# A decoder trunk's attention output projection: from four plain weight slots to the seven products of Strassen's algorithm

## The chip, the cores and the metric

The kernel is one program on one NeuronCore of a Trainium2 chip. The metric is the device time of one execution in microseconds; several runs are taken and the median is shown. The profile is one further execution, recorded instruction by instruction. The engines are TensorE (PE: matmuls and transposes), VectorE (DVE), ScalarE (ACT), GpSimd (POOL) and SyncE (SP, which issues the loads). They run in parallel and wait for each other through semaphores.

## The reference, cut to what matters

Two layers over 512 rows of width 1024. Layer 0 has two head groups (sparse softmax attention `o_a`, gated linear attention `o_b`), layer 1 a convolution module. The change concerns the last line of layer 0; its result is normed and is the input of layer 1.

```python
h = rmsnorm(x, norm_even[i]);  proj = h @ w_in_even[i]
...
o_a = dsa_attention(...).reshape(B, S, A_W) * jax.nn.silu(ga)      # 512 x 512
o_b = (rms-normed gla(...) * gla_norm).reshape(B, S, B_VW) * jax.nn.silu(gb)   # 512 x 512
x = x + jnp.concatenate([o_a, o_b], axis=-1) @ w_out_even[i]      # (512 x 1024) @ (1024 x 1024)
...
h = rmsnorm(x, norm_odd[j])
proj = h @ w_in_odd[j]
val, glu_g, gate = _split(proj, ODD_SPLIT)
```

## The kernel before, in words

Matmuls are made in three passes of rounded 32-bit operands: each operand is split into a high part (its rounding) and a low part (the rest), and high x high, high x low and low x high are summed in PSUM. So every weight has to be split before use. Weights come in slots of 1 MB (128 partitions x 2048 columns), listed by `plan_slots` (line 86) and numbered j. For each slot SyncE loads `w_raw[j % 2]` (`load`, line 452: it waits until the low part of slot j - 2 is made), ScalarE rounds it into `w_hi[j % 3]` (`split_hi`, line 729: it waits until TensorE has done with slot j - 3), and GpSimd subtracts into `w_lo[j % 3]` (`split_lo`, line 568). Each engine has its own program in a fixed order; nothing overtakes.

Slots 0 to 15 are the even layer's input projection, with the attention's and the linear attention's work put in between by hand. GpSimd's loop over slots (line 672) also holds the differences of the gated attention's levels (`diff`, line 630; levels "k", 64, 32, ...), which ScalarE exponentiates and VectorE multiplies for TensorE.

Slots 16 to 19 (`S_OE` up to `S_ODD`) are the output projection: two column halves of 512, each in two slots of 512 rows of the weight. First TensorE transposes the mixed rows `oa`, `ob` (32 blocks of 128x128, line 1529), ScalarE and VectorE make their high and low parts from PSUM (`hT_high`, `hT_low`), and then `unit_b` (line 1614) makes 12 matmuls of 128x512 for each of four row tiles in each slot. VectorE adds a finished tile to x (`add_rows`, line 1337), ScalarE takes squares (`row_squares`, line 896), VectorE makes the variance, GpSimd the reciprocal root (`rsqrt`, in its loop at step 19 ahead of the split of slot 21), VectorE scales the rows (`scale_rows`). TensorE transposes row tiles 0 and 1 of the normed x (`odd_rows(0)`, 16 transposes) before the very last unit of slot 19, and tiles 2 and 3 within the first odd slot, 20. That slot's matmuls (`group_half`, line 1890) wait chunk by chunk for the low parts of those rows, which follow the high parts (`half_high`, line 747).

GpSimd's order around the stage: split of 18, of 19, of 20 (the first odd slot), four `rsqrt`, a wait for all normed rows, split of 21.

## Time and profile before

| | us |
|---|---|
| median of 3 runs (lowest to highest) | 517.46 (517.19 to 517.59) |
| the profiled execution | 517.29 |
| its span, first to last instruction | 515.6 |
| TensorE matmul busy | 505.2 (98%), 2855 instructions |
| VectorE, ScalarE, GpSimd busy | 358.7, 244.6, 295.6 |
| mean granted TensorE clock | 0.998 of full |

The span is what the profile's rows cover; 1.69 us of the execution lie outside it. A busy TensorE is not one at its peak, as matmuls are pipelined: the distance between starts tells their cost.

### The profile page before, as it was taken

The page shows a single profiled execution, that of the slowest core. Times are in us where ns is not written, and L with a number is a line of the kernel's source. Part 1 is how long each engine was busy: PE and PEld are TensorE (multiplying, and loading weights), DVE is VectorE, ACT ScalarE, POOL GpSimd, SP SyncE. Part 2 cuts the span into 40 slices and gives each one's busy share as a digit, 9 for nine tenths or more (in the row PEclk, how much of TensorE's full clock was granted, in tenths as well). Part 3 has the DMA queues.
Part 4 walks back from the last instruction along what each step waited for, and adds up shares of the span by engine and source line. Part 5 has one row for each costly group of instructions (what it writes and reads, how often), then busy time and mean ns, then how long its engine had stood idle before and what let it go on. Part 6 is the DMA issues. An engine that isn't in the chain of part 4 may idle for free.

```text
span 515.6 us, 7658 instructions
## 1 busy us (share of the span) xinstructions
PE 505.2 (98%) x2855; PEld 408.0 (79%) x2855; DVE 358.7 (70%) x742; ACT 244.6 (47%) x407; POOL 295.6 (57%) x184
## 2 busy tenths in 40 slices
PE   7999999999999999999999999999999999999994
PEld 7866888788888888888898889888677777788883
DVE  3795599759966556647470136699999999849814
ACT  6734844232221244554271335648666665447303
POOL 5470755737734067556506404797999999950701
PEclk9999999999999999999999999999999999999999
DMA  8443355222222002100082220636877763502004
GB/s 272 116 153 124 123 164 164 84 83 83 83 73 92 1 0 83 51 32 1 10 317 83 82 82 0 164 83 158 203 195 184 185 162 106 175 31 81 1 0 163
DMA packets 47474, 54.73 MB, mean 106 GB/s; under 512 B 4424, under 2 KB 32099, under 8 KB 47438
## 3 DMA queue, kind: packets, MB, share of 16 engines
q1 hardware_dynamic: 47438, 54.25, 35.4%
q8 instruction: 22, 0.36, 0.3%
q14 instruction: 14, 0.11, 0.1%
HBM read 50.37 MB, written 3.72 MB: 105 GB/s over the span
## 4 chain that ended last, share of the span: by engine, by line
PE 86%; DVE 9%; ACT 3%; issue 1%; POOL 0%; POOLq 0%; ACTq 0%
PE bank L1608 33%; PE bank L1628 29%; PE bank L1826 3%; PE bank L1753 3%; DVE r_va L1147 2%; PE bank L1803 2%; PE bank L1917 2%; DVE top L1145 2%; PE bank L1904 2%; PE bank L1815 2%; DVE r_ob L1131 1%; PE bank L1644 1%; PE bank L1543 1%; PE bank L1692 1%; PE bank L1770 1%
## 5 line engine op out<-in xcount | busy, mean ns | idle before, releaser
L577 POOL TENSOR_TENSOR w_lo<-w_raw,w_hi 128x2048 fp32r<-128x2048 f32 (+1 forms) x31 | 140.4, 4529 | 99.6 <-ACT w_hi L739 98.6
L1608 PE MATMUL bank<-hT_lo,w_hi 128*128 128x512 f32 (+1 forms) x280 | 110.7, 395 | 0.0
L1608 PE MATMUL bank<-hT_hi,w_hi 128*128 128x512 f32 (+1 forms) x280 | 110.4, 394 | 0.0
L1608 PE MATMUL bank<-hT_hi,w_lo 128*128 128x512 f32 (+1 forms) x280 | 110.1, 393 | 0.0
L1628 PE MATMUL bank<-w_hi,hT_hi 128*128 128x512 f32 x252 | 101.9, 404 | 0.0
L1628 PE MATMUL bank<-w_hi,hT_lo 128*128 128x512 f32 x252 | 98.4, 391 | 0.0
L1628 PE MATMUL bank<-w_lo,hT_hi 128*128 128x512 f32 x252 | 98.3, 390 | 0.0
L739 ACT ACTIVATE w_hi<-w_raw 128x2048 fp32r<-128x2048 f32 (+1 forms) x35 | 65.7, 1880 | 40.3 <-PE bank L1628 35.3
L1401 DVE SCALAR_TENSOR_TENSOR bank<-r_va,pvec,bank 128x512 f32<-128x512 f32 x94 | 69.1, 753 | 2.2
L1608 PEld LDWEIGHTS bank<-hT_lo,w_hi 128*128 128x128 f32 (+1 forms) x280 | 52.3, 187 | 16.3 <-issue 5.7
L1608 PEld LDWEIGHTS bank<-hT_hi,w_hi 128*128 128x128 f32 (+1 forms) x280 | 52.3, 187 | 12.8 <-issue 1.5
L1608 PEld LDWEIGHTS bank<-hT_hi,w_lo 128*128 128x128 f32 (+1 forms) x280 | 52.3, 187 | 11.8 <-issue 1.0
L1628 PEld LDWEIGHTS bank<-w_hi,hT_hi 128*128 128x128 f32 x252 | 47.4, 188 | 11.9 <-issue 2.2
L1628 PEld LDWEIGHTS bank<-w_hi,hT_lo 128*128 128x128 f32 x252 | 47.3, 188 | 10.1
L1628 PEld LDWEIGHTS bank<-w_lo,hT_hi 128*128 128x128 f32 x252 | 47.4, 188 | 8.6
L658 POOL TENSOR_TENSOR r_g<-r_g 128x512 f32<-128x512 f32 x40 | 50.5, 1296 | 5.5 <-ACT r_g L938 5.5
L609 POOL TENSOR_TENSOR r_g<-r_x,neg_mask 128x128 f32<-128x128 f32 (+3 forms) x32 | 25.4, 798 | 39.7 <-DVE row_max L1257 36.6
L791 ACT ACTIVATE r_g<-r_g,neg_max 128x128 f32<-128x128 f32 (+3 forms) x32 | 17.9, 561 | 48.4 <-PE bank L1815 38.6
L1401 DVE SCALAR_TENSOR_TENSOR bank<-r_qkb,pvec,bank 128x512 f32<-128x512 f32 x48 | 35.2, 753 | 1.0
L565 POOL TENSOR_TENSOR rstd<-stat,minus_half 128x1 f32<-128x1 f32 (+1 forms) x13 | 9.6, 743 | 44.6 <-DVE stat L1044 40.3
L1282 DVE COPY r_g<-bank 128x128 f32<-128x128 f32 (+3 forms) x32 | 15.7, 491 | 22.1 <-PE bank L1815 21.9
L1340 DVE TENSOR_TENSOR r_x<-bank,r_x 128x512 f32<-128x512 f32 x8 | 5.5, 689 | 29.8 <-PE bank L1628 29.8
(240 smaller groups left out, 793.4 us busy)
## 6 DMA issues: line engine op xcount, KB each, us to landing
w_raw<-in_w_in_even_dram SPq DMA_DIRECT2D x14, 1024.0 KB, 5.2
w_raw<-in_w_in_odd_dram SPq DMA_DIRECT2D x16, 512.0 KB, 5.1
w_raw<-in_w_out_even_dram SPq DMA_DIRECT2D x4, 1024.0 KB, 8.3
w_raw<-in_w_in_odd_dram SPq DMA_DIRECT2D x4, 1024.0 KB, 7.9
w_raw<-in_w_out_odd_dram SPq DMA_DIRECT2D x4, 1024.0 KB, 5.0
r_att<-u_kept SPq DMA_DIRECT2D x12, 258.0 KB, 4.3
r_ka<-u_kept SPq DMA_DIRECT2D x12, 258.0 KB, 4.5
r_x<-in_x_dram SPq DMA_DIRECT2D x4, 512.0 KB, 6.0
```

The costliest lines, as they stand in the source:

```text
L577: nc.gpsimd.tensor_tensor(v(w_lo[j % 3]), v(w_raw[j % 2]), v(w_hi[j % 3]).bitcast(F32), ALU.subtract).then_inc(lo_ready, 1)
L609: nc.gpsimd.tensor_tensor(masked[n % 2][:, 0:w], bias_cols(h, w), neg_mask[:, MASK_AT[tb]:MASK_AT[tb] + w], ALU.add).then_inc(masked_ready, 1)
L658: nc.gpsimd.tensor_tensor(acc[i % 2], acc[i % 2], prod[((POOL_TAPS - 2) * c + i) % 3], ALU.add).then_inc(pool_added, 1)
L739: nc.scalar.activation(v(w_hi[j % 3]), v(w_raw[j % 2]), ACT.Copy).then_inc(hi_ready, 1)
L791: nc.scalar.activation(prob[n % 2][:, 0:w], logit[n % 2][:, 0:w], ACT.Exp, bias=neg_max[:, n:n + 1], accum_out=row_sum[:, n:n + 1]).then_i ...
L1145: ins = nc.vector.max(top8[:, tb - 1, :], score[tb])
L1282: nc.vector.tensor_copy(probT[n % 2][:, 0:w], bank[6][:, 0:w]).then_inc(probT_ready, 1)
L1401: ins = nc.vector.scalar_tensor_tensor(out=acc, in0=u, scalar=w, in1=acc, op0=ALU.mult, op1=ALU.add)
L1608: ins = nc.tensor.matmul(proj_bank(g)[0:m, :], w[:, k, P * i:P * i + m], h[:, k, :], start=(n == 0), stop=(n == 3 * KC - 1))
L1628: ins = nc.tensor.matmul(proj_bank(g)[:], h[:, k, P * t:P * t + P], w[:, i, :], start=(first and i == 0 and q == 0), stop=(final and i == ...
L1753: ins = nc.tensor.matmul(bank[4 + (n + i) % 4][:, n_q * t:n_q * t + n_q], keys, queries, start=True, stop=True)
L1826: ins = nc.tensor.matmul(bank[7][:, AD * h:AD * h + AD], probT[n % 2][:, P * i:P * i + P], va[:, i, AD * h:AD * h + AD], start=(i == 0), s ...
```

## The change

The rows are divided into an early half (tiles 0 and 1) and a late half (tiles 2 and 3), the columns into a (`oa`) and b (`ob`), and `w_out_even` into four quadrants B11, B12, B21, B22 of 512x512. Strassen's algorithm in its form with few sums, with some signs turned, makes seven products of 256x512 by 512x512 where four pairs (eight) were made: late b x B11, late a x B21, s1 x (B11 + B12), s2 x (B11 + B12 + B22), s3 x (B12 + B22), early a x (B11 + B12 + B21 + B22), s4 x B22, with s3 = late b - early b, s2 = - early a - s3, s1 = - s2 - late b, s4 = s1 - late a + late b. They accumulate in banks 2, 3, 6 and 7, and VectorE adds a bank to, or subtracts it from, tiles of x 14 times where there were 8 additions. Each product is a slot: 16 to 22. The odd layer's slots move from 20 to 23 and so on; `S_ODD` is 23.

The four sums of weights are made in device memory: SyncE copies quadrants (DRAM to DRAM), GpSimd issues six transfers that add onto them. Slots 18 and 19 are loaded from there to `w_raw`; slots 20, 21 and 22 (two sums and B22) go to `r_att`, `r_qa` and `r_ka`, early. The load of x moves behind slot 19's. The high parts of s1 to s4 are ScalarE's; the low parts of s3 and s1 are GpSimd's, between its splits of slots 18 and 19; the other sums and low parts are VectorE's. Only slot 16's and 17's splits stay within the attention. The order of the odd norm is rewritten: the squares of six half tiles stand between ScalarE's splits, and the four `rsqrt` stand behind GpSimd's split of slot 23. The diff, cut to its core:

```diff
+MIX = ("late b", "late a", "s1", "s2", "s3", "early a", "s4")
...
-    s += b("oe", 0, B_FIRST) + b("oe", 512, B_FIRST)
+    s += [("s", up[4:8], [(0, "oe", 0, 512)]), ("s", up[0:4], [(0, "oe", 0, 512)]), ("t", up[0:4], [(0, 0, 0, 512)]),
+          ("t", up[0:4], [(0, 1, 0, 512)])] + [("t", (), [])] * 3
...
+    B11, B12, B21, B22 = (WSRC["oe"][r:r + 512, c:c + 512] for r, c in ((512, 0), (512, 512), (0, 0), (0, 512)))
...
+        def raw(j):
+            if S_OE + 4 <= j < S_ODD:
+                return (r_att, r_qa, r_ka)[j - S_OE - 4][:, 0:2048]
...
+                if kind == "t":
+                    for _, n, _, _ in pieces:
+                        sp.wait_ge(lo_ready, j - 1)
+                        load_quadrant(w_raw[j % 2][:], t_sum[n], t_summed[n], (16, 32)[n], raw_in[j % 2])
+                    return
...
+                if j == 5:
+                    for i, q in enumerate((B11, B11, B12, B11)):
+                        sp.dma_start(t_sum[i], q).then_inc(t_begun, 16)
...
+                if j == S_OE + 3:
+                    sp.wait_ge(logit_ready, NSTEP)
+                    sp.dma_start(x_t, x[0].rearrange("(t p) d -> p t d", p=P)).then_inc(x_again, 16)
+                    sp.wait_ge(qk_done, NSTEP)
+                    load_quadrant(r_qa[:], t_sum[3], t_summed[3], 32, late_in[1])
+                    sp.dma_start(r_ka[:, 0:2048].rearrange("p (k n) -> p k n", k=4),
+                                 B22.rearrange("(k p) n -> p k n", p=P)).then_inc(late_in[2], 16)
...
+            def add_to(n, src):
+                nc.gpsimd.dma_start(t_sum[n], src, accum_op=ALU.add).then_inc(t_summed[n], 16)
...
+            def low_of_s3():
+                pool.wait_ge(mix_hi, 7)
+                pool.wait_ge(s2_ready, 2)
+                nc.gpsimd.tensor_tensor(s3_lo, s3, s3_hi.bitcast(F32), ALU.subtract).then_inc(s_low, 1)
+            def low_of_s1():
+                pool.wait_ge(mix_hi, 8)
...
-                if s_ == S_OE + 3:
+                if s_ == S_OE + 1:
+                    low_of_s3()
+                    low_of_s1()
+                if s_ == S_ODD - 1:
                     for t in range(TB):
...
+                if s_ == 3:
+                    pool.wait_ge(t_begun, 64)
+                    add_to(0, B12)
+                    add_to(1, B12)
+                    add_to(2, B22)
+                    add_to(3, B21)
+                if s_ == 5:
+                    pool.wait_ge(t_summed[2], 16)
+                    pool.wait_ge(t_summed[1], 16)
+                    pool.wait_ge(t_summed[3], 16)
+                    add_to(1, B22)
+                    add_to(3, t_sum[2])
...
+            for n in range(2):
+                act.wait_ge(mixed_T, n + 1)
+                nc.scalar.activation(hT_hi[:, 4 + 2 * n:6 + 2 * n, HALF:S], two_chunks(n), ACT.Copy,
+                                     scale=b_norm).then_inc(mix_hi, 1)
+                nc.scalar.activation(late_b[:, 512 * n:512 * n + 512], bank[n][:], ACT.Copy,
+                                     scale=b_norm).then_inc(late_kept, 1)
+            for n in range(2):
+                act.wait_ge(mixed_T, 5 + n)
+                nc.scalar.activation(hT_hi[:, 2 * n:2 * n + 2, 0:HALF], two_chunks(4 + n), ACT.Copy).then_inc(mix_hi, 1)
+            split_hi(S_OE + 2)
+            for n in range(2):
+                act.wait_ge(mixed_T, 7 + n)
+                nc.scalar.activation(hT_hi[:, 2 * n:2 * n + 2, HALF:S], two_chunks(n), ACT.Copy).then_inc(mix_hi, 1)
+            act.wait_ge(s3_ready, 2)
+            nc.scalar.activation(s3_hi, s3, ACT.Copy).then_inc(mix_hi, 1)
+            split_hi(S_OE + 3)
+            act.wait_ge(s1_ready, 2)
+            nc.scalar.activation(hT_hi[:, 4:KC, 0:HALF], s1.rearrange("p (c t) -> p c t", c=4), ACT.Copy).then_inc(mix_hi, 1)
+            for n in range(2):
+                cols = slice(512 * n, 512 * n + 512)
+                nc.scalar.activation(s2_hi[:, cols], bank[4 + n][:], ACT.Copy).then_inc(mix_hi, 1)
+            split_hi(S_OE + 4)
+            act.wait_ge(s4_ready, 4)
+            for n in range(2):
+                cols = slice(512 * n, 512 * n + 512)
+                nc.scalar.activation(s4_hi[:, cols], bank[n][:], ACT.Copy).then_inc(mix_hi, 1)
+            split_hi(S_OE + 5)
...
+            mix_square(2, 0, 0, 3)
+            mix_square(3, 0, 1, 4)
+            split_hi(S_OE + 6)
+            mix_square(0, 1, 2, 9)
+            mix_square(1, 1, 3, 10)
+            split_hi(S_ODD)
+            mix_square(0, 0, 4, 11)
+            mix_square(1, 0, 5, 12)
+            split_hi(S_ODD + 1)
+            mix_square(2, 1, 6, 13)
+            act.wait_ge(mix_unit, 12)
+            half_high(R_ODD, 0, odd_bank, odd_row)
+            mix_square(3, 1, 7, 14)
+            half_high(R_ODD, 1, odd_bank, odd_row)
...
+            def mix_add(b, t, half, unit):
+                dve.wait_ge(mix_unit, unit)
+                xs = x_t[:, t, 512 * half:512 * half + 512]
+                nc.vector.tensor_tensor(xs, xs, bank[b][:], ALU.subtract if half else ALU.add).then_inc(mix_added, 1)
...
+                dve.wait_ge(mixed_T, 3 + n)
+                nc.vector.scalar_tensor_tensor(out=s3[:, cols], in0=bank[2 + n][:], scalar=minus_norm, in1=late_b[:, cols],
+                                               op0=ALU.mult, op1=ALU.add).then_inc(s3_ready, 1)
+            for n in range(2):
+                low_of_chunks(4 + n, slice(2 * n, 2 * n + 2), EARLY, 3 + n)
+            for n in range(2):
+                cols = slice(512 * n, 512 * n + 512)
+                dve.wait_ge(s3_ready, n + 1)
+                dve.wait_ge(mix_low, 3 + n)
+                nc.vector.scalar_tensor_tensor(out=bank[4 + n][:], in0=bank[4 + n][:], scalar=-1.0, in1=s3[:, cols],
+                                               op0=ALU.mult, op1=ALU.subtract).then_inc(s2_ready, 1)
+            for n in range(2):
+                low_of_chunks(n, slice(2 * n, 2 * n + 2), LATE, 5 + n)
+            for n in range(2):
+                cols = slice(512 * n, 512 * n + 512)
+                dve.wait_ge(s2_ready, n + 1)
+                nc.vector.scalar_tensor_tensor(out=s1[:, cols], in0=bank[4 + n][:], scalar=-1.0, in1=late_b[:, cols],
+                                               op0=ALU.mult, op1=ALU.subtract).then_inc(s1_ready, 1)
+            for n in range(2):
+                cols = slice(512 * n, 512 * n + 512)
+                dve.wait_ge(s1_ready, n + 1)
+                dve.wait_ge(mix_low, 5 + n)
+                nc.vector.tensor_tensor(bank[n][:], s1[:, cols], bank[n][:], ALU.subtract).then_inc(s4_ready, 1)
+            for n in range(2):
+                cols = slice(512 * n, 512 * n + 512)
+                dve.wait_ge(s4_ready, n + 1)
+                nc.vector.tensor_tensor(bank[n][:], bank[n][:], late_b[:, cols], ALU.add).then_inc(s4_ready, 1)
+            dve.wait_ge(x_again, 16)
+            mix_add(6, 2, 0, 1)
+            for n in range(2):
+                cols = slice(512 * n, 512 * n + 512)
+                low_of_bank(4 + n, s2_lo[:, cols], s2_hi[:, cols], 9 + n)
+            mix_add(7, 3, 0, 2)
+            dve.wait_ge(mix_added, 2)
+            mix_add(2, 2, 0, 3)
+            mix_add(3, 3, 0, 4)
+            mix_add(2, 0, 1, 5)
+            for n in range(2):
+                cols = slice(512 * n, 512 * n + 512)
+                low_of_bank(n, s4_lo[:, cols], s4_hi[:, cols], 11 + n)
+            mix_add(3, 1, 1, 6)
+            mix_add(6, 2, 1, 7)
+            mix_add(7, 3, 1, 8)
+            dve.wait_ge(mix_added, 6)
+            mix_add(6, 0, 1, 9)
+            mix_add(7, 1, 1, 10)
...
+            def mix_variance(t):
+                last = 1 if t >= 2 else 0
+                dve.wait_ge(half_squares, 5 + t)
+                nc.vector.scalar_tensor_tensor(out=stat[:, t:t + 1], in0=half_sq[:, TB * last + t:TB * last + t + 1],
+                                               scalar=1.0 / D, in1=stat[:, t:t + 1], op0=ALU.mult,
+                                               op1=ALU.add).then_inc(var_ready, 1)
...
+            mean_square(2)
+            mean_square(3)
+            mix_add(6, 0, 0, 11)
+            mean_square(0)
+            mean_square(1)
+            mix_variance(0)
+            mix_add(7, 1, 0, 12)
             scale_rows(0, TB + 1)
-            row_variance(1, 0, 1)
+            mix_variance(1)
             scale_rows(1, TB + 2)
+            dve.wait_ge(mix_added, 8)
+            mix_add(2, 2, 1, 13)
...
+            FREED = {"s2": 1, "s1": 3, "s3": 7, "early a": 9, "s4": 5}
...
+                if name == "late a":
+                    pe.wait_ge(s3_ready, 2)
+                elif name in FREED:
+                    pe.wait_ge(mix_added, FREED[name] + t)
+                b = bank[MIX_BANK[name] + t]
+                wh = w_hi[j % 3][:].rearrange("p (k n) -> p k n", k=4)
+                wl = w_lo[j % 3][:].rearrange("p (k n) -> p k n", k=4)
+                pe.wait_ge(mix_hi, HIGH[name])
+                for q in range(3):
+                    if q == 1:
+                        slot_ready(j)
+                    if q == 2:
+                        if name in LOW:
+                            pe.wait_ge(mix_low, LOW[name])
+                        else:
+                            pe.wait_ge(s_low, LOW_S[name])
+                    for i in range(4):
+                        hi, lo = mix_operand(n, i, t)
+                        ins = nc.tensor.matmul(b[:], lo if q == 2 else hi, (wl if q == 1 else wh)[:, i, :],
+                                               start=(n < 3 and q == 0 and i == 0), stop=(q == 2 and i == 3),
+                                               skip_group_check=True)
+                ins.then_inc(mix_unit, 1)
...
+            quad_transposes(4, 2, 0)
+            quad_transposes(4, 0, 2)
+            pe.wait_ge(mixed_a, 1)
+            quad_transposes(0, 0, 4)
...
+            for n in range(len(MIX)):
+                pe.wait_ge(hi_ready, S_OE + n)
+                for t in range(2):
+                    if n == 0 and t == 1:
+                        pe.wait_ge(mix_low, 2)
+                        pe.wait_ge(late_kept, 2)
+                        pe.wait_ge(mixed_a, 2)
+                        quad_transposes(0, 2, 0)
+                        pe.wait_ge(oa_emptied, TB)
+                    if n == len(MIX) - 1 and t == 1:
                         odd_rows(0)
-                    unit_b(s_, t, hT_base=R_MIX if s_ < S_OE + 2 and t == 0 else None)
+                    mixed_unit(n, t)
```

## Rows read from the trace of the kernel before

**Rows 1.** The page, parts 1 and 4: busy us (share) by engine, and the chain's shares.

```profile
PE 505.2 (98%) x2855; PEld 408.0 (79%) x2855; DVE 358.7 (70%) x742; ACT 244.6 (47%) x407; POOL 295.6 (57%) x184
...
PE 86%; DVE 9%; ACT 3%; issue 1%; POOL 0%; POOLq 0%; ACTq 0%
```

**Rows 2.** The chain that ended last, in order of time: start us, us, what.

```profile
263.29 3.50 PE bank L1533 x32
266.79 40.83 PE bank L1628 x180
310.24 0.87 DVE hT_lo L1058 x2
313.73 3.59 PE bank L1904 x27
```

**Rows 3.** Timeline of GpSimd: start us, us, engine, line, operation [idle before].

```profile
271.07 4.60 POOL L577 TENSOR_TENSOR w_lo<-w_raw,w_hi 128x2048 fp32r<-128x2048 f32 x1 [16.99 <-ACT w_hi L739]
290.67 4.62 POOL L577 TENSOR_TENSOR w_lo<-w_raw,w_hi 128x2048 fp32r<-128x2048 f32 x1 [6.27 <-ACT w_hi L739]
304.01 0.56 POOL L565 TENSOR_TENSOR rstd<-stat,minus_half 128x1 f32<-128x1 f32 x1 [8.71 <-DVE stat L1044]
306.66 0.55 POOL L565 TENSOR_TENSOR rstd<-stat,minus_half 128x1 f32<-128x1 f32 x1 [2.09 <-DVE stat L1044]
```

**Rows 4.** Timeline of ScalarE, the changed stretch.

```profile
264.81 2.42 ACT L744 ACTIVATE hT_hi<-bank,pb 128x512 fp32r<-128x512 f32 x4 [2.96 <-PE bank L1533]
269.02 1.98 ACT L739 ACTIVATE w_hi<-w_raw 128x2048 fp32r<-128x2048 f32 x1
309.39 3.01 ACT L751 ACTIVATE hT_hi<-bank,pvec 128x256 fp32r<-128x256 f32 x8
```

**Rows 5.** Timeline of VectorE, the changed stretch.

```profile
264.67 0.69 DVE L1313 TENSOR_TENSOR r_oa<-r_oa,r_qkb 128x512 f32<-128x512 f32 x1
268.18 2.48 DVE L1050 SCALAR_TENSOR_TENSOR hT_lo<-bank,hT_hi 128x512 fp32r<-128x512 f32 x4
305.55 0.47 DVE L1032 TENSOR_SCALAR r_oa<-r_x,rstd 128x512 f32<-128x512 f32 x1
```

**Rows 6.** Timeline of GpSimd at the start: splits of 1024 columns.

```profile
9.07 2.38 POOL L614 TENSOR_TENSOR w_lo<-w_raw,w_hi 128x1024 fp32r<-128x1024 f32 x1 [1.09 <-ACT w_hi L766]
11.90 2.90 POOL L614 TENSOR_TENSOR w_lo<-w_raw,w_hi 128x1024 fp32r<-128x1024 f32 x1 [0.45 <-ACT w_hi L770]
```

**Rows 7.** Line 464's loads (two each): landing times, 275-277 and 320.5-324 us.

```profile
DMA to landing us min/median/max: 4.0/4.6/5.2
...
DMA to landing us min/median/max: 3.8/5.1/6.4
```

**Rows 8.** Timelines of VectorE (three rows), GpSimd and TensorE, 87 to 120 us.

```profile
90.20 2.11 DVE L1167 COPY chunk_decay<-r_oa 128x8 f32<-128x8 f32 x1
110.65 0.66 DVE L1178 TENSOR_TENSOR r_g<-r_g,r_qkb 128x512 f32<-128x512 f32 x1
118.72 1.86 DVE L1178 TENSOR_TENSOR r_g<-r_g,r_qkb 128x512 f32<-128x512 f32 x1
...
87.67 4.62 POOL L577 TENSOR_TENSOR w_lo<-w_raw,w_hi 128x2048 fp32r<-128x2048 f32 x1 [5.76 <-ACT w_hi L739]
...
96.42 0.66 PE L1719 MATMUL bank<-ident,r_g 128*128 128x128 f32 x4 [0.43 <-DVE r_g L1175]
```

**Rows 9.** Page part 6, timeline of ScalarE, and line 1753's instructions, 100 to 120.

```profile
w_raw<-in_w_in_even_dram SPq DMA_DIRECT2D x14, 1024.0 KB, 5.2
...
84.24 0.60 ACT L756 ACTIVATE r_vb<-bank 128x512 f32<-128x512 f32 x1 [2.12 <-PE bank L1628]
...
L1753 PE MATMUL bank<-r_g x32: 272/272/320, 114.6 to 116.4; 64*128 64x64 f32 x32
```

**Rows 10.** Stretches of the start: busy us by engine, granted clock, DMA, GB/s.

```profile
0.00:2.00 2.00, 0.00 (x0) 0.00 (x0) 0.27 (x1) 1.21 (x1) 1.05 (x9) 1.00 0.19 23
2.00:4.00 2.00, 1.31 (x13) 1.34 (x14) 0.29 (x1) 0.08 (x1) 1.31 (x7) 1.00 0.86 320
```

More of the change, by code:

```diff
@@ L148, in sb, with shared @@
             return ctx.enter_context(nc.sbuf_tensor(name, shape, dt))
+        def shared(name, shape):
+            with nc.sbuf_tensor(name, shape, F32) as plain:
+                pass
+            return plain, sb(name + "_split", shape, F32R)
         def sem(name):
@@ L271, in hybrid_trunk @@
         u_kept = nc.dram_tensor("u_kept", [2, P, KEPT], F32, kind="Internal").ap()
+        t_kept = nc.dram_tensor("t_kept", [2, 512, 1024], F32, kind="Internal").ap()
+        t_sum = [t_kept[i // 2][:, 512 * (i % 2):512 * (i % 2) + 512] for i in range(4)]
         bias_rows = nc.dram_tensor("bias_rows", [AH, S + P], F32, kind="Internal").ap()
@@ L286, in hybrid_trunk @@
         x_again = sem("x_again")
+        t_begun = sem("t_begun")
+        t_summed = [sem(f"t_summed{i}") for i in range(4)]
+        late_in = [sem(f"late_in{i}") for i in range(3)]
+        mixed_T = sem("mixed_T")
+        mix_hi = sem("mix_hi")
+        mix_low = sem("mix_low")
+        s_low = sem("s_low")
+        late_kept = sem("late_kept")
+        s1_ready = sem("s1_ready")
+        s2_ready = sem("s2_ready")
+        s3_ready = sem("s3_ready")
+        s4_ready = sem("s4_ready")
+        mix_unit = sem("mix_unit")
+        mix_added = sem("mix_added")
         nf_in = sem("nf_in")
@@ L1528, in _ @@
             pe.wait_ge(pool_chain, 2)
-            def transpose_blocks(order, blocks, ready, bank_of):
-                for n, t in blocks:
-                    ready(n, t)
-                    ins = nc.tensor.transpose(bank[bank_of(n)][:, P * t:P * t + P], hx(t, order[n]), ident[:])
-                    if t == TB - 1:
-                        ins.then_inc(hT_in_bank, 1)
-            LOW, HIGH = range(4), range(4, KC)
-            ROWS_1 = [(n, t) for part in (LOW, HIGH) for t in range(TB) for n in part]
             def keep_clock(n, dst):
@@ L1617, in unit_b @@
                 ks = SLOTS[j][1]
-                first, final = j % 2 == 0, j % 2 == 1
+                first, final = j in BEGINS, j not in BEGINS
                 if first and part[0] == 0:
@@ L1860, in _, with quad_transposes @@
             pv(NSTEP - 1)
[L1862 to L1871 removed]
+            def quad_transposes(first_chunk, first_t, first_bank):
+                for n in range(2):
+                    for c in range(2):
+                        for t in range(2):
+                            at = HALF * c + P * t
+                            ins = nc.tensor.transpose(bank[first_bank + n][:, at:at + P],
+                                                      hx(first_t + t, first_chunk + 2 * n + c), ident[:])
+                    ins.then_inc(mixed_T, 1)
```

168 lines of the change are left out of this document (96 added, 72 removed).

## The prediction

> **What bounds the kernel now.** I read the page first: TensorE is busy 98% of the span and holds 86% of the chain that ended last [rows 1]. So time is lost or won where TensorE's instructions are fewer, or where it is made to wait. Next the chain of waits over the changed stretch [rows 2]: 32 transposes take 263.29 to 266.79 us, then matmuls of 128x512 run without a gap. 180 of them take 40.83 us, so one costs 0.2268 us. The stretch ends with a wait on VectorE: the low part of the odd layer's transposed rows is late, and TensorE resumes at 313.73. Third, the timelines of the other engines. GpSimd splits a weight slot in 4.60 us and has long pauses [rows 3]; ScalarE splits one in 1.9 to 2.0 us and starts the odd layer's high parts at 309.39 [rows 4]; VectorE's 512-column step costs 0.69 us, and 0.62 from start to start when nothing is waited for [rows 5]. Slots here are numbered as in the plan; slot 23 after the change is what slot 20 was (the odd layer's first).
>
> **TensorE's saving.** Before: 4 slots x 4 row tiles x 12 = 192 matmuls. After: 7 products x 2 tiles x 12 = 168. The 32 transposes and the 16 of the odd rows stay. So 24 x 0.2268 = 5.44 us less, if nothing waits. A product takes 24 x 0.2268 = 5.44 us, and a slot serves TensorE for 5.44 us where it served 10.9: the other engines get half the time for each slot, and three slots more.
>
> **The start.** The first transposes begin at 263.1 (the chain gives 263.29, as it counts them from the end of the matmuls before). ScalarE may start a copy of a bank about 0.25 us after its last transpose was due, as at 264.81 [rows 4]. Six copies at 0.55 us follow (high and kept late b, twice; high early a, twice), 263.8 to 267.1, then the split of slot 18 to 269.0. Product 1 needs the second high part (265.5), so it starts at 265.8, as soon as 24 transposes are out; its second tile follows the last 8 transposes and ends at 272.1. Product 2 ends at 277.55. Its low parts are ready in time (271.9 against 274).
>
> **A first wait, about 1.5 us.** Product 3 starts anew in bank 2, so TensorE waits until VectorE has made its third addition to x. VectorE's queue from 265.3: 2 lows, 2 of s3, 2 lows, 2 of s2, 2 lows, 2 of s1, 4 of s4, one addition, 2 lows, 2 additions, 21 steps. At 0.62 us each, with a pause of 0.25 for ScalarE's second kept copy and 0.1 for each of two own waits, they end at 278.8. TensorE resumes at 279.0 instead of 277.55. Bounds: 0.9 us if no step pauses (265.3 + 13.0 = 278.3), 3.5 us if each takes 0.74, a whole 0.69 and a latency (280.8). I take the low side, since steps that don't wait for the one before start 0.62 apart in the rows. Beyond 2.3 us this wait would also push GpSimd's queue, below.
>
> **The wait that decides: GpSimd's queue before the odd rows.** The rsqrt of each row of the odd norm stands in GpSimd's order behind the split of the odd layer's first slot (23), as it did before behind slot 20, which was done at 290.67 + 4.6 [rows 3], 9 us early. Now the queue is: slot 18 (from 269.1), low of s3, low of s1, slots 19, 20, 21. Weight splits are 4.60; the two lows are 128x1024, of which the trace has one at 2.38 and one at 2.90 [rows 6]; I take 2.38, as nothing else holds the port there. 269.1 + 4.6 + 2 x 2.35 + 3 x 4.6 = 292.2. The high parts it needs come in time: slot 20's after product 2 (279.8), slot 21's after product 3, which ends at 284.5 (286.8, GpSimd free 287.6). Only when slot 21 is split does SyncE load slot 23, since a load waits for the low part two slots back. Two pieces of 512 KB, issued 0.5 us apart; the second lands 5.2 us after issue in the one row and 6.4 in the other [rows 7]. With 5.2 (three other odd slots have 5.1 to 5.4): 292.3 + 0.5 + 5.2 = 298.0. ScalarE splits it to 300.0, GpSimd to 304.7. Meanwhile products 4 to 6 end at 289.9, 295.35 and 300.8, and the first tile of product 7 at 303.5; there TensorE turns to the odd rows and must wait for them.
>
> One step more. VectorE's mix_variance(0) reads three operands in SBUF at about 300.8, while GpSimd splits slot 23. The trace shows that such steps wait for a running GpSimd instruction: the copy of 128x8 of line 1167 starts at 90.20, takes 2.11 us and ends where GpSimd's split of 87.67 + 4.62 ends, and the same kind of multiplication takes 0.66 us at 110.65, where GpSimd pauses, and 1.86 at 118.72, under a split [rows 8]. So mix_variance(0) and the addition queued behind it (number 12, which ScalarE's square and the norm of row 1 wait for) go at 304.7. The Trainium skill ("SBUF — State Buffer", Who interferes with whom) says the same: VectorE with two SBUF inputs and a GpSimd instruction that reads SBUF take turns on a shared port, and whichever came first blocks the other. By that rule my end is 0.3 us later than if the two could overlap.
>
> So: rsqrt(0) 304.9 to 305.5; addition 12 to 305.5; square to 306.4; scaling of row tile 0 to 306.4; variance, rsqrt(1) to 307.3 (0.6 us each, [rows 3]); scaling of row tile 1 (0.40 a half, [rows 5]) to 308.2. TensorE's 16 transposes end at 308.8 instead of 305.25: a second wait of 3.55 us. Its last tile ends at 311.5, which no longer matters, since the odd layer waits for VectorE and ScalarE: addition 13 at 308.8, its square to 309.6, then the high parts of the odd rows from 309.6, where they began at 309.39 before [rows 4]. From there the order is as before, and TensorE resumes at 313.9 against 313.73 [rows 2].
>
> The sum of the stage: -5.44 + 1.5 + 3.55 = -0.4 at TensorE's last tile (311.5 against 311.9), and then +0.6, because the low parts are waited for: +0.2 us.
>
> **The additions in device memory.** SyncE issues four 1 MB copies behind slot 5's load (at 39 us); GpSimd then adds onto them four times (behind slot 5's split, 64.75), waits for three of the four behind its split of slot 7, and issues two more. No row shows a copy from DRAM to DRAM or an addition. Copies: slot 6 is loaded at 58.1, behind them, and TensorE wants it when slot 5 is done, about 84 (its last bank is emptied at 84.24 [rows 9]); less two splits it may land as late as 77.5, so they may take till 72, 33 us for four. A load alone is 5.2 us [rows 9]; four make 21, and 42 if a copy costs a load and a store. Queued back to back a megabyte goes in 3.3 us (320 GB/s in [rows 10]), so 13, or 26 for load and store. The nearest row is a queue of loads, so I take the copies as hidden; at 42 slot 6 would land at 86 and TensorE lose 8 us, which belongs to rival 3. Additions: each reads two megabytes and writes one. If each costs two of those 3.3 us, four cost 26 and the slots' own loads 7: done near 98. If each costs three, near 111. GpSimd's split of slot 8 (87.67 [rows 8]) and the difference for level 64 stand behind that wait; TensorE wants the level at 114.6 [rows 9] and it needs 10 us from the release (split 4.6, difference 2.1, exponential 1.1, two products 1.3, latencies), so the breaking point is 104. I take no loss, with a rival for the other end. There is a gain too: if GpSimd's splits leave 90 to 96 us, the blocked copy and multiplications of VectorE there go quicker, and TensorE's wait of 0.43 us at 96.42 [rows 8] is gone. Take -0.4 (bounds 0 and -0.9, the weight load's wait there). The issues themselves: 0 to 1 us each of GpSimd, in pauses of about 5 us (5.8 before slot 8's split). The Trainium skill ("DMA: Bandwidth & Descriptors", Issuing engines are not separate DMA queues) has the additions share the 16 engines with SyncE's loads; no row here shows it.
>
> The one VectorE step for the minus sign (0.15 us in its pause) and SyncE's earlier wait for ob_summed (190 us, next load at 197.8) are free.
>
> **Sum.** 517.29 (profiled execution, 515.6 of span and 1.69 around it) + 0.2 - 0.4 = 517.1; the median shown is 0.17 higher, so 517.3.
>
> **The rivals.**
> 1. GpSimd's queue is not the end that decides (its steps run quicker, or another order). Then the variances follow the additions: rsqrt(1) near 303.6, high parts from 306.1 instead of 309.39: -3.3, 514.0. For it: before, slot 20's low part was there 9 us early. Against: each term is a row. 0.22.
> 2. Nothing waits at all, 5.44 less: 511.9. Against it are 21 VectorE steps in one queue. 0.04.
> 3. Slower: additions in device memory hold GpSimd beyond 104 us. Price: the time over 104, one for one; at three loads' cost 111, so 7 us; I write 521.3 for a typical 4. For it: the least known rate of all. 0.17.
> 4. Slower: both uncertain ends of the queue are the long ones, lows of 2.90 (+1.0) and a landing of 6.4 (+1.2): 519.4. 0.07.
> 5. Slower: the clock. TensorE idles about 2.6 us before the odd rows. The longest idle before has 2.7 us, at the very start, and the granted clock reads 1.00 there [rows 10]. If it fell to 1.2 GHz, the last tile would cost 2.7 us more, of which 2.3 are covered by the wait for the low parts; with a few half-speed matmuls of the odd layer +1.5: 518.8. 0.08. The Trainium skill ("TensorE: Matmul & The Clock Gate", Part 1) says that throttled is the default and activity releases it; by that rule such a gap is a risk.
> 6. The forecast, with its own range of 516.2 to 518.6: 0.42.
>
> **Numbers.** A difference under 0.2%, 1.0 us, is what a measurement of this kernel can't tell from none. The forecast's 0.42 is 0.36 within, 0.03 on either side. Faster 0.22 + 0.04 + 0.03 = 0.29; slower 0.17 + 0.07 + 0.08 + 0.03 = 0.35; same 0.36. The range runs from just below rival 1 to rival 3's typical price: 513.8 to 521.5.
>
> **What would show it.** TensorE: 168 matmuls of the mix, a wait of 1 to 2 us before product 3 released by VectorE's addition to x, and one of 3 to 4 us before the odd transposes, released by a scaling that waited for rsqrt, behind GpSimd's split of slot 23. GpSimd without a pause from 269 to 292. The high parts of the odd rows at 309.6 relative to transposes at 263.1. Wrong if the odd rows' transposes follow product 7's first tile at once, if GpSimd's split of slot 8 starts after 104, or if the granted clock falls below 1.00 in the stretch.

## The result, and the profile after

The changed kernel takes 533.39 us (median of 4 runs, 532.96 to 534.05) against 517.43 beside it: a ratio of 1.031, 95% interval 1.0297 to 1.0323, so 15.96 us slower. The forecast was 517.3, and its range ended at 521.5. The profiled execution has a span of 531.7 us against 515.6.

The page first, parts 1 and 4, as in [rows 1]: TensorE has 24 matmuls less and 95% instead of 98% of the span, and DMA stands in the chain, where it had no share.

```profile
PE 504.1 (95%) x2831; PEld 405.5 (76%) x2831; DVE 369.8 (70%) x761; ACT 254.0 (48%) x416; POOL 319.5 (60%) x195
...
PE 75%; DMA 8%; POOL 6%; ACT 4%; issue 3%; DVE 2%; SPq 0%; POOLq 0%; ACTq 0%; DVEq 0%
```

Where that share lies, the chain of waits shows for 60 to 120 us (start us, us, what). One addition in device memory takes 33.39 us, and everything until TensorE's matmul at 112.55 hangs on it.

```profile
66.64 33.39 DMA t_kept<-in_w_out_even_dram
...
101.22 1.41 POOL t_kept L673
102.63 4.52 POOL w_lo L636
107.15 0.99 POOL r_g L723
108.14 1.02 POOL r_g L724
109.18 1.06 ACT r_g L873
110.27 0.69 DVE r_g L1304
110.96 0.60 DVE r_g L1305
111.56 0.94 DVE r_oa L1315 x2
112.50 0.04 issue
112.55 1.12 PE bank L1930 x8
```

The same stretch in the timelines of the engines (idle time before an instruction, and what ended it, stand in brackets): TensorE, then GpSimd, then VectorE. VectorE's three steps at 90 us are those that were blocked in [rows 8].

```profile
112.55 1.12 PE L1930 MATMUL bank<-r_vb,r_oa 128*64 128x128 f32 x8 [14.13 <-DVE r_oa L1315]
```

```profile
100.58 1.01 POOL L673 DMA_DIRECT2D t_kept<-in_w_out_even_dram  x1 [18.80 <-DMA t_kept<-in_w_out_even_dram]
101.22 1.41 POOL L673 DMA_DIRECT2D t_kept<-t_kept  x1
101.87 5.28 POOL L636 TENSOR_TENSOR w_lo<-w_raw,w_hi 128x2048 fp32r<-128x2048 f32 x1
```

```profile
90.05 0.18 DVE L1293 COPY chunk_decay<-r_oa 128x8 f32<-128x8 f32 x1
90.26 1.23 DVE L1294 TENSOR_TENSOR r_oa<-r_oa,r_qkb 128x1024 f32<-128x1024 f32 x1
91.40 1.22 DVE L1301 TENSOR_TENSOR r_g<-r_g,r_qkb 128x1024 f32<-128x1024 f32 x1
110.27 0.69 DVE L1304 TENSOR_TENSOR r_g<-r_g,r_qkb 128x512 f32<-128x512 f32 x1 [17.65 <-ACT r_g L873]
111.48 1.01 DVE L1315 COPY r_oa<-bank 128x512 f32<-128x512 f32 x2
```

TensorE wants the copies of line 1315 (the k rows) at 98.4. Their data had been in the bank for a microsecond, but VectorE's list has level 64's operands (lines 1304 and 1305) ahead of them, and those need ScalarE's exponential, which needs GpSimd's difference, and ahead of that GpSimd has the split of slot 8 that stands behind the wait. Two things more can be read. By stretches (us, busy us by engine, granted clock, DMA share, GB/s) the clock falls to its half level of 1.2 GHz once TensorE has stood still, and stays there for the first 5 us of work:

```profile
98.00:103.00 5.00, 0.42 (x2) 0.00 (x0) 0.00 (x0) 0.00 (x0) 2.42 (x3) 0.84 0.55 147
...
113.00:118.00 5.00, 5.00 (x23) 3.31 (x20) 1.03 (x3) 0.00 (x0) 5.00 (x2) 0.50 0.77 226
118.00:123.00 5.00, 5.00 (x26) 3.35 (x25) 0.61 (x2) 1.55 (x2) 3.22 (x4) 0.96 0.66 210
```

The second: the traffic of the additions reaches slot 8's load, issued at 74.11. It lands after 19.9 us, where it took 5.2 at the same place before. ScalarE's high part, in the timeline, waits for it until 94.

```profile
94.02 1.92 ACT L834 ACTIVATE w_hi<-w_raw 128x2048 fp32r<-128x2048 f32 x1 [8.35 <-DMA w_raw<-in_w_in_even_dram]
```

The changed stage itself ends where it was forecast. Its transposes start at 279.19 (263.13 before) and those of the second pair of odd rows at 333.40 (317.16): 16.06 and 16.24 us later, so the stage costs 0.18 us. TensorE waits 0.84 us before product 3, and twice before the odd rows. The rows show GpSimd's split of slot 23, VectorE's 128x1 step of mix_variance(0), held by it on the shared port (below: the lock), GpSimd's square root and TensorE's two waits:

```profile
315.96 4.58 POOL L636 TENSOR_TENSOR w_lo<-w_raw,w_hi 128x2048 fp32r<-128x2048 f32 x1 [3.04 <-ACT w_hi L834]
316.59 3.98 DVE L1549 SCALAR_TENSOR_TENSOR stat<-half_sq,stat 128x1 f32<-128x1 f32 x1 [1.17 <-ACT r_qkb L1021]
320.64 0.56 POOL L624 TENSOR_TENSOR rstd<-stat,minus_half 128x1 f32<-128x1 f32 x1
321.78 0.66 PE L2132 MATMUL bank<-ident,r_oa 128*128 128x128 f32 x4 [1.89 <-DVE r_oa L1164]
323.39 1.12 PE L2132 MATMUL bank<-ident,r_oa 128*128 128x128 f32 x4 [0.52 <-DVE r_oa L1164]
```

### The profile page after: what moved, and what is told of

Read it like the earlier page. It is cut to its first block, busy times and chain, and to the rows that moved or that the text cites. A ratio compares the mean times of both kernels' runs of the same rounds, so it can differ in the third digit from the quotient of the medians.

```text
span 531.7 us, 7684 instructions
## 1 busy us (share of the span) xinstructions
PE 504.1 (95%) x2831; PEld 405.5 (76%) x2831; DVE 369.8 (70%) x761; ACT 254.0 (48%) x416; POOL 319.5 (60%) x195
## 4 chain that ended last, share of the span: by engine, by line
PE 75%; DMA 8%; POOL 6%; ACT 4%; issue 3%; DVE 2%; SPq 0%; POOLq 0%; ACTq 0%; DVEq 0%
PE bank L1809 32%; PE bank L1829 21%; DMA t_kept<-in_w_out_even_dram 6%; POOL w_lo L636 4%; PE bank L2027 3%; PE bank L1954 3%; PE bank L2004 2%; PE bank L2163 2%; PE bank L2176 2%; PE bank L2016 2%; PE bank L1845 1%; ACT w_hi L834 1%; PE bank L1893 1%; DMA w_raw<-in_w_in_odd_dram 1%; DMA r_x<-in_x_dram 1%
## 5 line engine op out<-in xcount | busy, mean ns | idle before, releaser
L1829 PE MATMUL bank<-w_hi,hT_hi 128*128 128x512 f32 x188 | 76.8, 409 | 0.0
L1829 PE MATMUL bank<-w_hi,hT_lo 128*128 128x512 f32 x188 | 73.5, 391 | 0.0
L1829 PE MATMUL bank<-w_lo,hT_hi 128*128 128x512 f32 x188 | 73.4, 391 | 0.0
L1829 PEld LDWEIGHTS bank<-w_hi,hT_hi 128*128 128x128 f32 x188 | 35.4, 188 | 9.5 <-issue 2.2
L1829 PEld LDWEIGHTS bank<-w_hi,hT_lo 128*128 128x128 f32 x188 | 35.3, 188 | 7.6
L1829 PEld LDWEIGHTS bank<-w_lo,hT_hi 128*128 128x128 f32 x188 | 35.4, 188 | 6.2
L1383 DVE CUSTOM_DVE_ANT_0 r_g<-bank,r_g 128x128 f32<-128x128 f32 (+3 forms) x32 | 15.6, 487 | 14.5 <-PE bank L2004 8.4
```

Source lines behind the costliest of these rows:

```text
L1383: nc.vector.tensor_tensor_reduce(out=logit[n % 2][:, 0:w], in0=bank[4 + n % 2][:, 0:w], in1=masked[n % 2][:, 0:w], scale=1.0, scalar=-3.0e ...
L1829: ins = nc.tensor.matmul(proj_bank(g)[:], h[:, k, P * t:P * t + P], w[:, i, :], start=(first and i == 0 and q == 0), stop=(final and i == ...
```

## The experiments

Each time has the kernel before beside it on the same chip (517.37 to 517.51). Four questions, in this order: is it GpSimd's wait or the traffic; where is the breaking point; what do the transfers cost and where do they fit; what holds the stage.

**Wait moved.** 

> The changed kernel, with GpSimd's wait for the first additions and its two further additions moved from step 5 of its loop to step 10, where it pauses anyway. All transfers are still made. Theory A (the loss is GpSimd's wait until 100 us, which holds back the split of slot 8 and the difference for level 64, and through VectorE's order TensorE): the 14.1 us wait of TensorE near 98 us and the slow clock after it go, and what is left is the stage, which I had at +0.2: 517 to 518 us. Theory B (the 14 MB of additional traffic slow the loads or the engines): 525 or more. Theory C (the seven products themselves cost several us): above 519.

```diff
-                if s_ == 5:
+                if s_ == 10:
                     pool.wait_ge(t_summed[2], 16)
```

525.17 us, ratio 1.0152 (95% interval 1.0137 to 1.0167): neither theory alone. TensorE's pause is 7.31 us instead of 14.13. GpSimd's split of slot 8 now starts at 95.87, behind ScalarE's high part at 93.87, which waits 8.11 us for the load, as above. So the wait was hiding a second delay, of 8 us against the 87.67 of [rows 8], made by the traffic.

```profile
105.83 1.12 PE bank L1930 x8
```

(The chain's piece at which TensorE goes on, here, against 112.55 above.)

**Copies first.** 

> The changed kernel; GpSimd waits as before until about 100 us. Only VectorE's order differs: the five copies and state updates that TensorE wants near 98 us stand ahead of the multiplication for level 64, which waits for GpSimd's difference. Theory A1 (my breaking point of 104 us was right for level 64's own use, and wrong only because the copies are queued behind that multiplication): TensorE's 14.1 us wait goes, 517 to 519 us. Rival A2 (the next thing in line, the split of slot 8 or ScalarE's emptying of slot 6 behind the exponential, is late as well): a rest of 3 us or more stays, 520 to 530.

```diff
             operand("k")
-            operand(64)
-            for f in FILLS[0:5] + level(0):
+            for f in FILLS[0:5]:
+                empty_fill(f)
+            operand(64)
+            for f in level(0):
                 empty_fill(f)
```

524.97, 1.0145 (1.0128 to 1.0162). The pause at 98 is gone with wait and traffic both in place, so the order of VectorE's list is what let GpSimd's wait reach TensorE. What is left is the next place of the same kind: level 64's copies stand behind level 32's operands, which GpSimd brings late, so that TensorE waits 4.01 us until 125.62 and finds the clock down (0.59 in 123 to 128, 0.75 in 128 to 140). The work at that lower clock costs as much again: the block at 125.62 starts 3.40 us later than before, the one at 137.18 7.36 us. For level 64 itself, which TensorE wants at 113.94 here, there is no wait, though slot 8's split started at 101.27: that level alone does not contradict the forecast's 104.

**Delay only.** 

> The kernel before, with eleven small power operations (about 1.7 us each, 19 us together) in GpSimd's queue at the place where the changed kernel waits; no transfer in device memory, no products changed. Theory A: TensorE waits some 13 to 15 us near 98 us and restarts at half the clock: 531 to 534 us. Theory B (traffic): 518 to 520, as 104 us were thought to be the breaking point and this delay ends near 101.

```diff
+                if s_ == 5:
+                    for _ in range(11):
+                        link(nc.gpsimd.tensor_tensor(rstd[:, 8:16], ones[:, 0:8], minus_half[:, 0:8], ALU.pow))
```

531.93, 1.0280 (1.0264 to 1.0295): the kernel before with nothing of the change but a busy GpSimd loses 14.4 of the 16 us.

**Clock kept.** 

> The changed kernel, with 230 small bf16 matmuls (about 56 ns each, 12.9 us) on TensorE just ahead of its 14.1 us wait, so that it waits 1.2 us only and the clock stays up. The window after the wait ran 6 us at 1.2 GHz, which cost about 2.5 us. Theory: 530 to 531.5 us, 2 to 3 less. Rival (the slow clock costs nothing since something else is late): 533.4 as it was.

```diff
                 if f[:2] == "kv":
+                    if t == 0:
+                        keep_clock(230, bank[7])
                     pe.wait_ge(fill_emptied, FILL_NO["k1"] + 1)
```

530.61, 1.0253 (1.0238 to 1.0269). TensorE works through the pause at a granted clock of 1.00, and the kernel is 2.8 us faster than the changed one: about that much of the 16 is matmuls at half speed after the pause (2.6 by the rows of the account below).

**Middle delay.** 

> The kernel before, with 7 extra steps of 128x8 powers on GpSimd (near 12 us, no transfer) where the changed kernel has its wait, at the end of step 5; 11 of them cost 14.4 us. Theory (the breaking point is where GpSimd begins slot 8's split, 87.7): the split begins 4 to 5 us late, 521 to 523. Rival (the point is 104, as predicted; only a delay beyond it costs): 517.5.

As the delay alone, with range(7). 525.24, 1.0149 (1.0136 to 1.0162). Each step took 1.85 us instead of the 1.7 I had put, so GpSimd was held for 12.95 us, not 12, and the split of slot 8 starts 7.24 us late. GpSimd's split and TensorE's pause, first in the middle, then in the long delay:

```profile
94.91 4.58 POOL L577 TENSOR_TENSOR w_lo<-w_raw,w_hi 128x2048 fp32r<-128x2048 f32 x1
104.90 1.12 PE L1732 MATMUL bank<-r_vb,r_oa 128*64 128x128 f32 x8 [6.35 <-DVE r_oa L1192]
```

```profile
101.84 4.49 POOL L577 TENSOR_TENSOR w_lo<-w_raw,w_hi 128x2048 fp32r<-128x2048 f32 x1
111.75 1.12 PE L1732 MATMUL bank<-r_vb,r_oa 128*64 128x128 f32 x8 [13.12 <-DVE r_oa L1192]
```

Late by 7.24 us it costs 7.8, late by 14.2 it costs 14.4. The pause follows the split's start one for one and goes to nothing at 88.6 (94.91 less 6.35) and 88.7 (101.84 less 13.12). That is the breaking point, 0.9 us behind the undelayed start of 87.67, and not 104. What a run loses beyond its pause is lost at the lowered clock (0.56 in 103 to 108, 0.76 in 108 to 113 in the middle delay). The time is above my 521 to 523 because the delay was longer and because I had left out the clock.

**Plain copies** (the six transfers of GpSimd don't add, so the weight sums aren't made). 

> The changed kernel with GpSimd's six transfers as plain copies, without accumulation, so the weight sums are not made. Theory (the transfers' cost is the bytes: an addition reads twice and writes once, a copy reads and writes once): the wait of 18.8 us shrinks by about a third of the transfers' 33 us, to 8 or 9, TensorE's pause is 5 to 8 us and the time 522 to 527. Rival 1 (the way of the transfers, not the second read, costs): the wait stays over 16 us and the time over 531. Rival 2 (accumulation costs far more than its bytes): no wait is left, under 519.

```diff
-                nc.gpsimd.dma_start(t_sum[n], src, accum_op=ALU.add).then_inc(t_summed[n], 16)
+                nc.gpsimd.dma_start(t_sum[n], src).then_inc(t_summed[n], 16)
```

520.18, 1.0052 (1.0039 to 1.0065): less than even the theory said. Landing times of GpSimd's transfers, changed kernel and this one:

```profile
DMA to landing us min/median/max: 9.4/16.8/33.4
```

```profile
DMA to landing us min/median/max: 7.9/11.8/18.8
```

The longest shrinks to 0.56 of itself, not to two thirds; GpSimd's wait is 3.8 us instead of 18.8, and slot 8's high part starts at 87.66 instead of 94.02. A pause of 2.3 us is left to TensorE, at 98.41 and for another reason: it waits for VectorE's multiplication of line 1301. An issue costs GpSimd 0.62 us instead of 1.46.

**Later transfers.** 

> The changed kernel with the same transfers issued later: the four copies behind slot 12's load (near 137 us), the four additions behind GpSimd's step 10 (near 152 to 167), the wait for them and the last two additions at step 12 (near 200). Theory (the whole loss is the wait and the traffic at 65 to 100, and the rest of the change is worth what was forecast): no pause of TensorE at 98, slot 8's high part at 85 to 86 as before, 517.2 to 518.0. Rival (traffic costs wherever it stands, as it slows some load by 8 us or more, or the stage costs more than 0.2): 519 or more, with the pause at another product.

```diff
-                if j == 5:
+                if j == 12:
                     for i, q in enumerate((B11, B11, B12, B11)):
...
-                if s_ == 3:
+                if s_ == 10:
                     pool.wait_ge(t_begun, 64)
...
-                if s_ == 5:
+                if s_ == 12:
                     pool.wait_ge(t_summed[2], 16)
```

516.88, 0.9991 (0.9983 to 1.0): the whole loss is gone. The transfers are as slow as before (landing 10.3, 16.2 and 28.8 us), but TensorE waits for none of the loads that they slow at 120 to 215 us. The copies went out at 120.5; my 137 was read from the changed kernel's timeline, which runs 16 us late. TensorE's 0.4 us at 96 is back, with VectorE's three steps at 2.07, 2.02 and 2.01 us under the split of slot 8 (pieces of the chain):

```profile
90.31 2.07 DVE chunk_decay L1293
92.41 2.02 DVE r_oa L1294
94.42 2.01 DVE r_g L1301
```

**Both undone**, wait moved and copies first. 

> The changed kernel with two of the earlier edits together: the wait and the last two additions moved from GpSimd's step 5 to step 10, and VectorE's copies of the k rows placed ahead of level 64's operands; copies and first four additions where they were, so slot 8's high part stays 8 us late. Theory (TensorE's pause comes only from the order of VectorE's queue, and the 4.0 us that stayed with the copies first came from GpSimd's wait): level 64's operands are 6 us earlier than with the copies first, no wait of TensorE is left near 98 or 119, 517.2 to 518.5. Rival (the traffic's delay of slot 8 and of the bias table costs time by itself further on): 520 or more.

516.25, 0.9980 (0.9971 to 0.9988), a little better than the theory. Slot 8 is as late here as in the first experiment (split at 95.33), copies and additions run where the change put them, and TensorE has no pause between 84 and 250 us. It beats the later transfers by 0.6 us, since the late split leaves the port free at 90: the matmul that waited 0.43 us at 96.42 [rows 8] goes at once, and the one behind it, of the k rows' copies, starts at 98.57 instead of 99.14.

```profile
95.94 0.60 PE L1922 MATMUL bank<-ident,r_g 128*128 128x128 f32 x4
```

**Load early.** 

> As the kernel with the later transfers, and slot 23's load no longer waits for the split of slot 21 but for that of slot 19, the last reader of its buffer. Theory (the wait in front of the odd rows comes from the landing of that load through GpSimd's split and the port lock on the 128x1 step): load issued near 283 to 286 of its time, the split ends 2 to 3 us earlier, TensorE's waits of 1.9 and 0.5 us ahead of the odd rows go and the clock does not dip there: 1.5 to 3 us less than the kernel with the later transfers, 514.5 to 516.3. Rival (ScalarE's squares, which wait for the additions to x, are next at once): less than 0.5 us of gain, 517 or more.

```diff
-                    sp.wait_ge(lo_ready, j - 1)
+                    sp.wait_ge(lo_ready, (j - 3 if j == S_ODD else j - 1))
```

516.04, 0.9970 (0.9958 to 0.9981): 0.84 us better than the later transfers, about half of the least gain I expected, though the time lies within the range. The load is early, but ScalarE's list has a square ahead of slot 23's high part, and GpSimd's split moves by 0.75 us only (299.83 to 299.08).

**Square roots first.** 

> As the kernel with the later transfers, and GpSimd takes the first two rows' square roots ahead of slot 23's split instead of behind it. Theory (GpSimd's order is what holds the odd rows): the 128x1 step takes 0.15 instead of 4 us, the waits ahead of the odd rows go, slot 23's low part ends near 3.5 us later and just in time: 514.5 to 516.5. Rival (slot 23's low part becomes the bound): the gain is given back at the first product of the odd stage, 517 to 519.

```diff
+                if s_ == S_ODD - 2:
+                    for t in range(2):
+                        rsqrt(t, t + 1, var_ready, TB + t + 1, rstd_ready)
                 if s_ == S_ODD - 1:
-                    for t in range(TB):
+                    for t in range(2, TB):
```

518.44, 1.0026 (1.0015 to 1.0036): slower, by 1.6 us against the later transfers, and by neither of my ways. Its runs spread more than the others' (517.57 to 520.07), and the trace is of the fastest, so it shows where the wait went and not what the median lost. The 128x1 step does take 0.16 us, and row 0 follows without a wait. But now the split that stood ahead stands behind, and the lock holds the scaling of row 1 instead, for which TensorE waits 3.45 us. GpSimd and VectorE:

```profile
303.27 4.52 POOL L636 TENSOR_TENSOR w_lo<-w_raw,w_hi 128x2048 fp32r<-128x2048 f32 x1
303.34 4.74 DVE L1167 TENSOR_SCALAR r_oa<-r_x,rstd 128x512 f32<-128x512 f32 x1 [0.66 <-POOL rstd L624]
```

**High part first**, on top of the early load. 

> As the kernel with the later transfers and slot 23's load early, and ScalarE makes slot 23's high part one square earlier, ahead of that of row 1's right half. Theory (with the load early it is ScalarE's order that holds the split, whose lock on the port holds the 128x1 step): the split starts near 297.6 instead of 299.1 and ends near 302.2, TensorE's wait of 0.9 us ahead of row 0 goes, row 1's stays near 0.5: 0.7 to 1.2 us less than with the load early alone, 514.9 to 515.4. Rival (the square put back holds the next steps as long): no gain, 516.0.

```diff
             mix_square(0, 1, 2, 9)
-            mix_square(1, 1, 3, 10)
             split_hi(S_ODD)
+            mix_square(1, 1, 3, 10)
```

514.71, 0.9951 (0.9939 to 0.9963). The split starts at 297.68 and ends where the step that it blocks is let go, early enough that row 0 follows at once. Of 2.3 us of waits ahead of the odd rows 0.41 is left. GpSimd, VectorE, TensorE:

```profile
297.68 4.61 POOL L636 TENSOR_TENSOR w_lo<-w_raw,w_hi 128x2048 fp32r<-128x2048 f32 x1 [0.82 <-ACT w_hi L834]
300.00 2.32 DVE L1549 SCALAR_TENSOR_TENSOR stat<-half_sq,stat 128x1 f32<-128x1 f32 x1 [0.61 <-ACT r_qkb L1021]
303.70 0.60 PE L2132 MATMUL bank<-ident,r_oa 128*128 128x128 f32 x4
```

**Quarters.** 

> As the kernel with the later transfers and slot 23's load early, and GpSimd makes slot 23's low part in four quarters of 128x512 with the first two rows' square roots between and behind them. Theory (one GpSimd instruction of 4.6 us holds the port for its whole length, so shorter ones let VectorE's 128x1 step in): that step takes under 1.5 us instead of 3.6, the wait of 0.9 us ahead of row 0 goes, 514.8 to 515.5. Rival (four quarters in a row lock the port as one does): 516.0 or more.

```diff
+                elif s_ == S_ODD - 2:
+                    quarter_lo(S_ODD, 0)
+                    quarter_lo(S_ODD, 1)
+                    rsqrt(0, 1, var_ready, TB + 1, rstd_ready)
+                    quarter_lo(S_ODD, 2)
+                    quarter_lo(S_ODD, 3)
+                    rsqrt(1, 2, var_ready, TB + 2, rstd_ready)
```

515.78, 0.9968 (0.9956 to 0.9980): 0.26 us less than with the early load, less than expected and too little to be told from none, as the intervals of the two overlap. The 128x1 step takes 0.27 us, so the lock is as long as GpSimd's instruction; but the next two quarters hold both scalings of row 0 at 1.5 us each, and 1.3 us of waits remain.

**All four edits** (wait moved, copies first, load early, high part first). 

> The changed kernel with four edits: GpSimd's wait at step 10, VectorE's copies of the k rows ahead of level 64's operands, slot 23's load after the split of slot 19, and slot 23's high part one square earlier; the copies and the first four additions stay near 40 and 65. Theory (the two regions are apart, so the savings add): 516.25 less the 2.17 us between the later transfers (516.88) and the same with load and high part early (514.71), 513.8 to 514.5. Rival (one stage's gain is lost in the other's): 514.7 or more.

514.04, 0.9938 (0.9924 to 0.9952), 5 runs from 513.98 to 514.54. It beats both kernels: 3.3 us under the kernel before and 19.4 under the changed one. The repairs of the two regions add up.

## Why the prediction was wrong

**The step that failed** is one sentence of the part on the additions: "so the breaking point is 104". The rate above it held, the lower of the two that it weighed: two megabyte times for each addition gave "done near 98", and they landed at 100.04. The copies were hidden, as taken: the last was issued at 40.8 and landed in at most 16.4 us, before slot 6's load at 57.97. What was wrong is the consumer that I worked back from. I looked for the first use of what stands behind the wait, level 64 at 114.6 [rows 9]. The first engine to suffer was another: VectorE waits in its own list for level 64's operands with the k rows' copies behind them, and TensorE wants those at 98. The prediction named the multiplications of VectorE there and never asked what is queued behind them. Its 10 us from the release to TensorE were right: 9.99 and 9.91 us lie between the split's start and TensorE's in the two delays. Worked back from 98.5 instead of 114.6 they give 88.6, 0.9 us behind the start of slot 8's split [rows 8]: next to no slack, and "I take no loss" was 14 us off.

**A second miss, hidden behind the first.** I counted the slots' own loads as 7 us of the additions' time and not the additions as time of the loads. Slot 8's load took 19.9 us for 5.2, slot 9's 22.4. By itself this costs 7.7 us (wait moved). It runs beside the wait, so the two don't add: 7.7 and 14.4 would make 22. The Trainium skill ("DMA: Bandwidth & Descriptors", Issuing engines are not separate DMA queues) has transfers of all engines interleave on the same 16 DMA engines. I cited it for the additions alone; these loads agree, and by that rule they had to be charged both ways.

**Rival 3** had the right mechanism with the wrong point: with a limit of 104 a split that starts at 101.87 costs nothing, and its price of 4 us was counted from there. The forecast's own test (wrong if slot 8's split starts after 104) did not catch it either. **Rival 5**, the clock, came true in two places. One is behind the long pause, 2.6 to 2.8 us. The other is ahead of the odd rows, where the rival had put it: the clock reads 0.50 from 324 to 326, after waits of 1.89 and 0.52 us with a few transposes between them. The wait for the low parts covers most of that, but not all. From the stage's first transposes to those of the second pair of odd rows it is 54.21 us here and 54.19 with the later transfers, both with this dip. With wait moved and with both undone, which leave the stage as it is, the clock reads 1.00 there, and it is 53.85 and 53.54.

**The gain of 0.4** from the free port is real: VectorE's three steps took 0.18, 1.23 and 1.22 us, and both undone ran without the wait of 0.43. In the changed kernel the pause behind it swallowed it.

**The stage**: +0.2 predicted, +0.18 measured, and that close a match is luck. Against 54.03 before, the stage without the dip is 0.2 to 0.5 us shorter; the clock, which the sum left out, took that back. Before product 3 the wait was 0.84 us, just under the lower bound of 0.9, not 1.5. Before the odd rows the chain was as described: slot 23's split ends 41.4 us after the stage's start, where I had 41.6, the lock holds the 128x1 step for 3.98 us until then, and TensorE is through with the transposes 45.8 us after the start (325.02), where I had 45.7. I had called all of this a wait of 3.55; the rows have 1.89 + 0.52 of waits and the rest as slower transposes. Rival 1's point, that the stage could end 3.3 us sooner without this queue, is borne out for 2.2 of them (high part first against the later transfers).

**The account**, by TensorE's rows. Before, the matmul that the pause holds back stands at 99.11:

```profile
99.11 0.66 PE L1729 MATMUL bank<-r_vb,r_oa 128*64 128x128 f32 x8
```

In the changed kernel it starts at 112.55, 13.44 us later. The first block of matmuls for the levels follows at 123.03 instead of 106.97, 16.06 later, so the lowered clock between the two costs 2.62; with the clock kept up both starts are 13.93 us late. Nothing is added until the stage (16.06), which adds 0.18; the medians differ by 15.96. The long delay alone has 12.64 at the first of these places and 14.13 at the second. Of the changed kernel's 1.9 us more, 0.8 comes ahead of the restart: right behind the two issues the split of slot 8 and the differences took 7.27 us in all, against 6.51 in the long delay and 6.56 in wait moved, where additions still ran when the split began but none had just been issued. The other 1.1 is clock, which stays low longer (0.50 against 0.79 in 113 to 118); why it does was not tested.

## What to carry to other kernels

Before a wait is put into an engine's queue, follow what is behind it through every in-order list that it feeds, not to the first use of the result but to the first thing that stands behind a step waiting for it; the breaking point is the earliest of these. A transfer that is off every engine still takes bandwidth from the loads that aren't: ask which load lands within its time, and put bulk work on device memory where none has to. And where one long GpSimd instruction meets many short VectorE ones, start it early; placed elsewhere, its lock only falls on another step.

## What the runs showed of the hardware

- Accumulating in device memory cost more than its bytes: 4 additions of 1 MB took up to 33.4 us from issue, the same transfers as plain copies up to 18.8. That is 1.8 times, where two reads and a write for one of each would give 1.5; the slots' own loads ran beside both. An issue kept GpSimd 1.46 us against 0.62.
- Four plain 1 MB copies from DRAM to DRAM on SyncE's queue took 8.6 to 16.4 us, where a load alone takes 5.2 [rows 9].
- A load of 1 MB into SBUF, issued by SyncE while GpSimd's additions ran, took 19.9 and 22.4 us instead of 5.2.
- What the clock costs behind a pause does not follow the pause's length: 4.0 us of work lost behind a pause of 4.01 (copies first), 2.5 behind 6.35, 1.3 behind 7.31, 1.5 behind 13.12, 2.6 behind 14.13. Each is by how much the start of a later block slipped against the restart.
- The port lock falls on tensor_scalar as well: 128x512 took 4.74 us for 0.48, until the split beside it had ended. The Trainium skill ("SBUF — State Buffer", Who interferes with whom) lists tensor_scalar among the operations that can take the shared pair, and says that a blocked engine blocks fully; both agree with these rows.
